# Ten modulation pieces summed by two engines beside the even layer's projection, and two weight requests moved to another program

## The reference

```
for layer in range(DEPTH):
    mod_l = jax.nn.silu(c) @ w_ada[layer] + b_ada[layer]
    mod_c = jax.nn.silu(c_ctx) @ w_ada[layer] + b_ada[layer]
    sh1, sc1, g1, sh2, sc2, g2 = [m[:, None, :] for m in jnp.split(mod_l, 6, axis=-1)]
    ...
    h_l = modulate(x_lat, g_mix[layer], sh1, sc1)
    h_c = modulate(x_ctx, g_mix[layer], sh1c, sc1c)
    if layer % 2 == 0:
        o_l, o_c = even_mixer(h_l, h_c, not last, e_w_in[j], e_w_out[j], e_g_q[j], e_g_k[j],
                              e_conv_w[j], e_conv_b[j], e_b_gates[j], e_g_h[j], rope_64)
```

## Time and profile before

| | |
|---|---|
| median of three executions | 3146.27 us (3143.32 to 3149.4) |
| the profiled execution | 3146.45 us |
| its span | 3144.5 us |
| TensorE busy | 2863.3 us, 91% of the span |
| VectorE, ScalarE, GpSimd busy | 47%, 34%, 22% |
| `modulation` | 0 to 41 us |
| `even_project` | 42 to 452 us |
| `even_mlstm` | 452 to 605 us |

### The profile page before, as it was taken

The page is one execution under the profiler, slowest core; times in us unless marked ns, Lnnn a source line. Parts: engine busy times, 40 slices in busy tenths (PEclk is TensorE's granted clock), DMA queues, the critical chain, the costliest instruction groups (busy, mean ns, idle before and its releaser), DMA issues. The chain is left out here.

```text
span 3144.5 us, 72871 instructions
## 1 busy us (share of the span) xinstructions
PE 2863.3 (91%) x27771; PEld 1889.6 (60%) x27771; DVE 1480.4 (47%) x4244; ACT 1082.9 (34%) x2480; POOL 692.9 (22%) x929
## 2 busy tenths in 40 slices
PE   6999988899999689999987999899999959998895
PEld 3666656745544357776663555577776537795573
DVE  2667436755554432222224677566665342232223
ACT  1222124466621123333333343455553103332232
POOL 0000005799051033332221010000002013332233
PEclk8999988899999899999998999899999979999998
DMA  9722027433052399999984221200003459999997
GB/s 371 276 91 77 20 102 231 116 112 100 1 181 88 158 376 414 413 416 417 418 355 155 84 82 66 74 1 1 1 1 116 154 222 384 418 416 417 418 417 300
DMA packets 167397, 665.00 MB, mean 211 GB/s; under 512 B 25373, under 2 KB 37929, under 8 KB 117621
## 3 DMA queue, kind: packets, MB, share of 16 engines
q1 hardware_dynamic: 136736, 574.30, 47.1%
q0 software_dynamic: 19456, 56.67, 5.1%
q10 hardware_dynamic: 10964, 30.68, 2.5%
HBM read 581.98 MB, written 86.90 MB: 213 GB/s over the span
## 5 line engine op out<-in xcount | busy, mean ns | idle before, releaser
L2877 PE MATMUL ps_g<-w_ring,work 128*32 128x256 f32 x7328 | 432.0, 382 | 26.5 <-DMA w_ring<-in_w 15.1
L2964 DVE STREAM_TRANSPOSE work<-work 128x256 f32<-128x256 f32 x189 | 123.6, 654 | 662.1 <-PE ps_g L2877 633.6
L2877 PEld LDWEIGHTS ps_g<-w_ring,work 128*32 128x32 f32 x7328 | 290.7, 110 | 138.5 <-issue 32.4
L2930 ACT COPY work<-ps_y 32x256 f32<-32x256 f32 x760 | 275.7, 363 | 285.0 <-PE ps_y L2892 278.2
L2877 PE MATMUL ps_g<-w_early,work 128*32 128x256 f32 x4640 | 281.4, 389 | 36.2 <-DMA w_early<-in_w 24.7
L2002 PE MATMUL of_ps_r<-w_early,cat 128*128 128x512 f32 (+1 forms) x608 | 255.9, 577 | 1.6 <-ACT cat L2084 1.6
L2877 PEld LDWEIGHTS ps_g<-w_early,work 128*32 128x32 f32 x4640 | 183.6, 112 | 113.3 <-issue 44.8
L484 PE MATMUL ps_r<-w,hT 128*128 128x512 f32 (+1 forms) x640 | 250.0, 547 | 1.5 <-ACT hT L554 1.5
L2825 POOL DMA_INDIRECT work<-f_dram,ex_idx x200 | 204.6, 1023 | 171.4 <-POOL ex_idx L2822 168.9
L2924 ACT ACTIVATE work<-ps_g 128x128 f32<-128x128 f32 x192 | 53.3, 277 | 515.8 <-PE ps_g L2877 509.1
L2892 PE MATMUL ps_y<-w_ring,work 128*32 128x256 f32 x3680 | 226.7, 380 | 3.4 <-ACT work L2930 3.4
(11 more groups left out here) (509 smaller groups left out, 4432.7 us busy)
## 6 DMA issues: line engine op xcount, KB each, us to landing
w_ring<-in_w SPq DMA_DIRECT2D x232, 1024.0 KB, 25.2
w_early<-in_w SPq DMA_DIRECT2D x152, 1024.0 KB, 25.4
y_dram<-work ACTq DMA_DIRECT2D x190, 128.0 KB, 5.9
y_dram<-zeros POOLq DMA_DIRECT2D x4, 4608.0 KB, 27.2
ea_slab<-in_w_ada SPq DMA_DIRECT2D x64, 256.0 KB, 2.9
zT<-in_w_ada SPq DMA_DIRECT2D x12, 1024.0 KB, 6.0
f_dram<-mo_f SPq DMA_DIRECT2D x18, 512.0 KB, 2.9
w<-in_e_w_in SPq DMA_DIRECT2D x2, 4096.0 KB, 20.4
```

The lines of the kernel that those rows point to most:

```text
L2877: mm = pe.matmul(ps_h[rows, :], xT[:, k * UNIT:(k + 1) * UNIT], w[:, :, kk * DE + n * P:kk * DE + (n + 1) * P], start=k == 0, stop=k == KD ...
L2930: w = act.copy(y[b * UNIT:(b + 1) * UNIT, n * 256:(n + 1) * 256], ps_y[n * UNIT:(n + 1) * UNIT, :])
L2964: dve.transpose(xT.rearrange("p (k t) -> p k t", k=KD), xs.rearrange("p (r k) -> p k r", k=KD)).then_inc(x_turned, 1)
```

## The change

Ten pieces (4 to 13, `SUMMED` = 10) are summed in `even_project` in place of six, two for each of the tiles 1 to 5. VectorE sums the latent kind only, a whole piece at each of its two places; GpSimd sums the context kind of the same slabs, behind its fill requests. GpSimd multiplies a slab by a column into `product` and adds that to its sum, each instruction waiting for the one before. A half of the slabs is requested again only when both engines have used it. VectorE has one running sum instead of two, so each of its instructions waits for the one before. The two kinds are stored by a request each, and the loads of later latent rows stand behind GpSimd's stores. In `even_mlstm` five units are left: sums of four, four and two pieces, and the whole pieces 14 and 15. Besides, the last two weight groups are requested at the head of the projection's SyncE program instead of the end of the modulation's.

```diff
-SUMMED = 6
+SUMMED = 10
...
-                for n, (at, (a, b), group) in enumerate(W_COLUMNS):
+                for n, (at, (a, b), group) in enumerate(W_COLUMNS[0:2]):
...
                 def slab_load(n, half):
+                    if n >= SUMMED:
+                        return
                     if n:
-                        sp.wait_ge(slab_used[half], n)
+                        sp.wait_ge(used_dve[half], n)
+                        sp.wait_ge(used_pool[half], n)
...
+                for at, (a, b), group in W_COLUMNS[2:]:
+                    sp.dma_start(L.w[:, :, at:at + b - a], A["e_w_in"][0, :, a:b].rearrange("(k p) n -> p k n", p=P)).then_inc(L.w_in[group], 16)
                 x_load(0)
                 slab_load(0, 0)
                 slab_load(0, 1)
                 x_load(1)
                 for n in range(SUMMED):
+                    slab_load(n + 1, 0)
+                    dve_store(n)
+                    slab_load(n + 1, 1)
+                    pool_store(n)
+                    if n % 2 == 0:
+                        x_load(n // 2 + 2)
...
+                for n in range(SUMMED):
+                    to = acc_pool[n % 2]
+                    for half in range(2):
+                        pool.wait_ge(slab_in[half], 16 * n + 16)
+                        if half == 0 and n > 1:
+                            pool.wait_ge(pool_st[n % 2], 16 * (n // 2))
+                        for k in range(4 * half, 4 * half + 4):
+                            pool.tensor_scalar(product if k else to, slabs[:, k, :], L.cs[:, k, 1:2], None, ALU.mult).then_inc(*pool_step.up())
+                            pool.wait_ge(*pool_step.now())
+                            if k:
+                                pool.tensor_tensor(to, to, product, ALU.add).then_inc(*pool_step.up())
+                                pool.wait_ge(*pool_step.now())
+                        pool.sem_inc(used_pool[half], 1)
                 pool.wait_ge(filled, 64)
...
-        units = [("sums", 0, 4)] + [("whole", q) for q in range(whole, whole + 3)] + [("sums", 4, SUMMED)] + [("whole", q) for q in range(whole + 3, LAST[0])]
+        units = [("sums", 0, 4), ("sums", 4, 8)] + [("whole", q) for q in range(whole, LAST[0])] + [("sums", 8, SUMMED)]
```

More of the change, by code:

```diff
@@ L588, in q_out @@
                     if h == 0 and not place_of(i, h)[0] and not place_of(i, h)[1]:
-                        act.wait_ge(acc_st, i * 32)
+                        act.wait_ge(dve_st, i * 64 - 32)
+                        for b in range(2):
+                            act.wait_ge(pool_st[b], i * 32 - 16)
                     act.wait_ge(qt_done, i * 2 + h + 2)
@@ L675, in channels_out, with summed @@
                         m.then_inc(z_dve, 1)
[L677 to L685, removed]
+                def summed(i, h, second):
+                    n = i * 4 + 2 * h - 2 + second
+                    for half in range(2):
+                        dve.wait_ge(slab_in[half], n * 16 + 16)
+                        if half == 0 and not (isinstance(n, int) and n == 0):
+                            dve.wait_ge(dve_st, n * 16)
+                        for k in range(4 * half, 4 * half + 4):
+                            by = L.cs[:, k, 0:1]
                             if k == 0:
-                                m = dve.tensor_scalar(acc[kind], slabs[:, k, :], by, None, ALU.mult)
+                                m = dve.tensor_scalar(acc, slabs[:, k, :], by, None, ALU.mult)
                             else:
-                                dve.wait_ge(*c.but(1))
-                                m = dve.scalar_tensor_tensor(out=acc[kind], in0=slabs[:, k, :], scalar=by, in1=acc[kind], op0=ALU.mult, op1=ALU.add)
+                                dve.wait_ge(*c.now())
+                                m = dve.scalar_tensor_tensor(out=acc, in0=slabs[:, k, :], scalar=by, in1=acc, op0=ALU.mult, op1=ALU.add)
                             m.then_inc(*c.up())
-                    dve.wait_ge(*c.now())
-                    dve.sem_inc(slab_used[half], 1)
+                        dve.wait_ge(*c.now())
+                        dve.sem_inc(used_dve[half], 1)
                 def k_out(i, h):
@@ L700, in tile @@
                     first, final, last, before, after = place_of(i, h)
-                    sums = not first and not (isinstance(i, int) and i * 2 + h > SUMMED)
+                    sums = not first and not (isinstance(i, int) and i * 2 + h > SUMMED // 2)
                     if sums:
@@ L727, in _ @@
                 tile(0, 1)
-                turns = SUMMED // 2 - 1
+                turns = SUMMED // 4
                 with dve.Fori(0, turns) as j:
@@ L832, in load @@
                         ada_load(sp, A, units[n][1], wa[buf(n)], ada_in[buf(n)])
-                for n in range(6):
+                for n in range(LATE):
                     load(n)
@@ L839, in _ @@
                 sp.dma_start(row_dram[1].rearrange("d r t -> (d r) t"), ai_row).then_inc(rows_out, 16)
-                for n in range(6, LATE):
-                    load(n)
                 sp.wait_ge(rows_out, 32)
@@ L1045, in _ @@
                     gate(cc)
-                    if cc < 6:
+                    if cc < LATE:
                         ada_out(cc)
-                for n in range(6, LATE):
-                    ada_out(n)
                 act.wait_ge(tabs_ready, 1)
```

51 lines of the change are left out of this document (25 added, 26 removed).

## The result

The changed kernel takes **3199.69 us** (median of four runs, 3197.83 to 3207.45) against 3147.84 of the kernel before (four runs, 3143.32 to 3149.56). That is 52 us slower by the medians; the ratio over all the runs is 1.0171, with a 95% interval of 1.0159 to 1.0183. I had forecast 3240 (93 slower), with a range of 3165 to 3300. Direction and place were right. The size was not: my own range for the forecast case began at 3208. In the run of the experiment sums and in one run of tt_late (5971 and 6368 us) TensorE's matmuls took about twice as long from the first stage to the last, and these two times are compared with nothing.

The account below looks back on a forecast made before the run. TensorE was taken to bound the projection (40 us a tile), loads the mLSTM's first part. First turn 24 plus four tiles' 80, less 11 in the mLSTM, gave +93: 3240 us, range 3165 to 3300.

Parts of the forecast that it names:

- the forecast case: Whole kernel: 3240 us, 93 slower, own range 3208 to 3267, chance 0.70.
- One sign that I had named: Projection: TensorE waiting at each turn of tiles 1 to 5, for VectorE or ScalarE.
- rival A: Projection: GpSimd's pace only, products by a column not holding up VectorE; 45.4 us a tile, 3177 us, chance 0.10.
- A tile with two pieces: Projection: GpSimd's and VectorE's instructions share one resource; 60 us a tile, 20 more than TensorE's 40.
- the first turn: Projection: the turn of tile 1 comes at 162.3 us instead of 138.2, 24 late.
- the fill: Start of projection: fourth request waits 47.8 us and ends at 120.1, fill beginning 1.1 us later; GpSimd's sums stand behind it.
- the last four sums: First turn: VectorE's sums, each with a GpSimd instruction between, take 7.5 us.
- The start: Start of projection: without the last two weight requests TensorE begins 4.3 us earlier, which vanishes in the wait at tile 1.
- The mLSTM: First part of the mLSTM: fewer bytes loaded, first scores 11 us sooner, with ends at 8 and 17.
- Rival D: Projection: GpSimd begins at about 70, ninth piece done at 274, nothing late; 15 us faster, 3131 us, chance 0.06.
- Rival B: Projection: cheap GpSimd products of 0.61 us, 15.1 us a piece, tile 45; 3170 us, chance 0.07.

Follow-up runs that it names:

- sums: Changed kernel, GpSimd doing 15 sums a piece and no products on its own buffers, nobody waiting for it: 5971 us, TensorE's matmuls about twice as long.
- tt_late: Changed kernel with GpSimd's fill requests behind its sums and its product made by a tensor_tensor with the column spread: ratio 1.0085 to the kernel before.
- Silent: Changed kernel without GpSimd's fifteen instructions of each piece; it only clears its sum once a piece, and all waits stay: 3145.72 us.
- free: Changed kernel, GpSimd doing the same mix of products and sums on three buffers of its own, nobody waiting for it: 3134.65 us.
- fill_late: Changed kernel with GpSimd's four fill requests put behind its sums: 3160.36 us, ratio 1.0041 to the kernel before.
- products: Changed kernel, GpSimd doing 15 products by a column a piece and no sums on its own buffers, nobody waiting for it: 3134.08 us.
- sums2: The run sums again (changed kernel, GpSimd doing only sums on its own buffers, nobody waiting): 3177.86 us.
- unmoved: Changed kernel with the last two weight requests back where they were: ratio 1.0161 to the kernel before.
- moved_only: Kernel before with only the last two weight requests moved into the projection's SyncE program: 3142.22 us against 3147.83, ratio 0.9983.
- tt_late2: The kernel of tt_late again (fill requests behind the sums, product with spread column), for a profile: 3172.7 us.

## Why the prediction was right, and where its size was wrong

**Direction, and the place: right.** GpSimd cannot keep TensorE's pace, VectorE is held by it through the half-slabs, and TensorE waits for VectorE from the turn of tile 1 to that of tile 5. Silent, free and fill_late show each link apart. One sign that I had named did not come: TensorE waits at the turn of tile 1 alone; after that it waits at the transposes (L488). That the time lies in the stated range is owed in part to its width, which took in rival A as well.

**"A tile with two pieces" is the step that failed.** I charged each of GpSimd's 16 products with 1.42 us of a port that VectorE cannot use meanwhile, came to 53.5 to 60.4 us, and took 60. The three tiles took 50.9, 50.6 and 51.1. A product by a column costs VectorE 0.22 us, a sum 0.67 (products, sums2). I had seen the sums and the products by a constant beside VectorE, and carried this over to the one instruction that no row showed beside it. The row that I held against rival A says less than I took from it: L1815 took 1.60 us beside a product by a constant of 0.61, but its median in the trace of before is 1.28, so that product cost it 0.32, about half of its record. What is left is GpSimd's own pace, slowed by VectorE: 25.1 us a piece in these tiles, where I had worked out 22.7 from undisturbed durations. So the mechanism is rival A's, with one thing that A left out: VectorE makes GpSimd's instructions longer, too (1.74 and 1.37 us in these tiles for 1.56 and 1.27). The tile lies between A's 45.4 and the forecast's 60. Over four tiles this is 80 forecast and 46.7 measured, and so 33 of the 41 us of the error; the first turn has the rest.

**The first turn: right in kind, 8 us too late in the forecast** (162.3 against 154.1). 5.2 of it is the fill: the fourth request was held 43.6 us and not 47.8 (in the other runs with the fill in its old place 43.3 to 50.3), and the fill began at 63.6 and not 1.1 us later. The other 3 are the last four sums: 4.4 us and not 7.5, the same price as above. The start came 5.2 us earlier and not 4.3; that it would vanish in this wait was right (unmoved).

**The mLSTM: 11 was right, to a microsecond or two, for a run with the clock up.** The distance to the first scores falls from 53.2 (53.4 in moved_only, with the same code) to between 40.4 and 41.4 us in seven traces, by 11.8 to 12.8. In the profiled run of the changed kernel it fell by 6.5 only, and in sums2 by 8.4, beside a lower granted clock. With 11.8 the sum would be 62.6 - 11.8 = 50.8 us, near the 52 of the medians; that the other three runs had this value was not seen, since only one of them has a trace.

**Rival D's condition was tried.** With GpSimd beginning when the first slab has landed (fill_late), the time is 1.0041 of before and not below it. The ninth piece ends at 301 us and not at 274: GpSimd waits 9.1 us for the slabs of its second piece, which D left out, since VectorE comes to the first one only in tile 1; and the eight pieces from there on take 25.3 us each and not 22.7.

**Rival B fell as forecast:** no product was near 0.6 us. The Trainium skill ("GPSIMD Engine Reference", section 4.1, Engine selection) has one-input work on GpSimd at about line rate; here the one-input product by a column took 1.72 us in its mean, longer than the two-input product with a spread column (1.18), so the trace speaks against it for this form.

## What to carry to other kernels

When two engines consume the same buffer, its reload comes at the slower one's pace: work out that engine's time for a piece, with the durations it has beside its neighbour, and compare it with the slot before anything else. A helper on GpSimd has two prices, the time it takes and the time it takes from VectorE, and they need not go together: here the longer instruction was the better neighbour, and VectorE alone did the whole work in 41.8 us a tile where the two together took 51 (its first tile took 49.8, and the whole was no faster than before: 1.0008). What stands ahead in the helper's queue decides when it begins: moving four requests that nobody needed yet behind its sums gave back 39 us.

## What the hardware showed that I had not expected

A product by a column of 128x512 on GpSimd takes 1.70 us in its mean and lengthens VectorE's work by 0.22 us; a sum takes 1.46 and lengthens it by 0.67; a product with the column spread takes 1.18, and is about as costly to VectorE as a sum: 0.64 is the mean of both kinds in tt_late2. In the timeline of the changed kernel three of VectorE's sums run beside one such product:

```profile
208.31 1.31 POOL L471 TENSOR_TENSOR qT<-qT 128x512 f32<-128x512 f32 x1
208.54 3.52 DVE L714 SCALAR_TENSOR_TENSOR qT<-zT,cs,qT 128x512 f32<-128x512 f32 x3
209.72 1.88 POOL L468 TENSOR_SCALAR qT<-zT,cs 128x512 f32<-128x512 f32 x1
```

If the first is held up until L471 ends at 209.62, all three are done at 212.06, in 2.44 us or 0.81 each; the product's 1.88 us lie in that time. Which part of a product's record keeps VectorE out, the records do not tell; the 0.22 is a mean over a tile.
